# A two-layer decoder trunk on one core: router logits summed by quarter, with edits at the late units, the gated unit and the end

## What is computed

```python
h = rms_norm(x, norm_mix[l]);  parts = split_columns(h @ w_in[l])       # 7176 columns
y_a = moba_attention(q, k, v) @ w_up_moba[l]                            # 8 heads of 64, causal
glu_a, glu_b = jnp.split(gelu(s5_ssm(u, ...)) @ ssm_w_glu[l], 2, axis=-1)
y_b = glu_a * sigmoid(glu_b)                                            # the gated unit
y_c = gated_delta_rule(...) @ w_up_gdn[l]
x = x + (sigmoid(gate_a)*y_a + sigmoid(gate_b)*y_b + sigmoid(gate_c)*y_c) @ w_out[l]
x = x + cross_attention(rms_norm(x, norm_xa[l]), rms_norm(mem, norm_mem[l]), ...)
h = rms_norm(x, norm_ffn[l])
# layer 0: x = x + swiglu(h, ...)
# layer 1, over 8 experts, D_FF = 2816:
logits = h @ w_router;  top_val, top_idx = top_k(logits, 2);  top_w = softmax(top_val)
x = x + sum_e comb[:, e] * swiglu(h, w_gate[e], w_up[e], w_down[e])
# behind the last layer: rms_norm(x, norm_final)
```

## Time and profile before

| | |
|---|---|
| Median of 3 runs | 1755.19 us (1753.54 to 1756.68) |
| The profiled execution's own time | 1754.76 us |
| Its span in the trace | 1753.0 us |
| PE busy | 1696.0 us, 97% |
| DVE busy | 1391.7 us, 79% |
| ACT busy | 1061.0 us, 61% |
| Memory traffic | 434.93 MB, mean 248 GB/s |

### The profile page before, as it was taken

How to read it: one execution, slowest core, us unless ns; L and a number is a source line. 1 busy time by engine, 2 the same in 40 slices (tenths; PEclk the granted TensorE clock), 3 DMA queues, 4 the chain that set the end, 5 groups by cost and what they waited for, 6 DMA issues and landing times. The chain is left out here.

```text
span 1753.0 us, 23683 instructions
## 1 busy us (share of the span) xinstructions
PE 1696.0 (97%) x9485; PEld 1376.7 (79%) x9485; DVE 1391.7 (79%) x1769; ACT 1061.0 (61%) x1228; POOL 160.8 (9%) x218
## 2 busy tenths in 40 slices
PE   8999999999999999999999999999999999999996
PEld 5777767788888888776778788888888888888885
DVE  5798678765555599857875799999998989899996
ACT  4235565565434523566556677777777777777865
POOL 7420002000000333000200100000000000000020
PEclk9999999999999999999999999999999999999998
DMA  8444433355651644453224699999999999999993
GB/s 266 144 145 162 174 119 131 125 192 193 215 173 66 210 145 145 149 187 106 88 101 173 245 395 377 395 372 395 372 396 367 396 387 377 390 374 389 361 395 131
DMA packets 220196, 434.93 MB, mean 248 GB/s; under 512 B 19180, under 2 KB 63864, under 8 KB 220088
## 3 DMA queue, kind: packets, MB, share of 16 engines
q1 hardware_dynamic: 213704, 419.45, 66.4%
q0 software_dynamic: 3520, 11.76, 1.7%
q10 hardware_dynamic: 2864, 2.23, 0.4%
HBM read 422.93 MB, written 10.49 MB: 247 GB/s over the span
## 5 line engine op out<-in xcount | busy, mean ns | idle before, releaser
L1666 DVE TENSOR_TENSOR split_e<-ring,split_e 128x2048 fp32r<-128x2048 f32 x264 | 598.5, 2289 | 40.2 <-ACT split_e L1078 39.9
L1078 ACT ACTIVATE split_e<-ring 128x2048 fp32r<-128x2048 f32 x264 | 503.8, 1921 | 148.7 <-PE bank L3197 127.7
L3195 PE MATMUL bank<-split_e,fx_e 128*128 128x512 f32 x704 | 278.6, 396 | 0.5 <-DVE fx_e L2470 0.5
L3197 PE MATMUL bank<-split_e,fx_e 128*128 128x512 f32 x704 | 274.7, 390 | 0.0
L3196 PE MATMUL bank<-split_e,fx_e 128*128 128x512 f32 x704 | 274.2, 390 | 0.0
L3197 PEld LDWEIGHTS bank<-split_e,fx_e 128*128 128x128 f32 x704 | 132.1, 188 | 28.1
L3195 PEld LDWEIGHTS bank<-split_e,fx_e 128*128 128x128 f32 x704 | 132.2, 188 | 26.7 <-DVE fx_e L2470 0.7
L3196 PEld LDWEIGHTS bank<-split_e,fx_e 128*128 128x128 f32 x704 | 132.4, 188 | 26.2
L3195 PE MATMUL bank<-split_e,f_actT_e 128*128 128x512 f32 x352 | 137.7, 391 | 1.2 <-DVE f_actT_e L2478 1.2
L3197 PE MATMUL bank<-split_e,f_actT_e 128*128 128x512 f32 x352 | 137.0, 389 | 0.0
L3196 PE MATMUL bank<-split_e,f_actT_e 128*128 128x512 f32 x352 | 137.0, 389 | 0.0
(11 more groups left out here) (645 smaller groups left out, 3299.4 us busy)
## 6 DMA issues: line engine op xcount, KB each, us to landing
ring<-in_moe_w_gate SPq DMA_DIRECT2D x40, 2048.0 KB, 13.1
ring<-in_moe_w_up SPq DMA_DIRECT2D x40, 2048.0 KB, 13.1
ring<-in_moe_w_down SPq DMA_DIRECT2D x40, 2048.0 KB, 13.4
ring<-in_w_in SPq DMA_DIRECT2D x27, 2048.0 KB, 8.0
ring<-in_ffn_w_gate SPq DMA_DIRECT2D x11, 1024.0 KB, 5.4
ring<-in_ffn_w_up SPq DMA_DIRECT2D x11, 1024.0 KB, 7.9
ring<-in_ffn_w_down SPq DMA_DIRECT2D x11, 1024.0 KB, 8.8
ring<-in_ssm_w_glu SPq DMA_DIRECT2D x8, 1024.0 KB, 6.2
```

The costliest lines, as they stand in the source:

```text
L1078: nc.scalar.activation(split_e[j % NBUF][:, HI, :], ring[:, s * PIECE + i * HGRP:s * PIECE + (i + 1) * HGRP], ACT.Copy).then_inc(split_hi, 1)
L1666: V.tensor_tensor(split_e[j % NBUF][:, LO, :], ring[:, s * PIECE + i * HGRP:s * PIECE + (i + 1) * HGRP], split_e[j % NBUF][:, HI, :].bitca ...
L3195: mm(bank, a[HI], w[HI], start=first, stop=False)
L3197: return mm(bank, a[LO], w[HI], start=False, stop=last_one)
```

## The change

It has five parts.

1. **Late units.** ACT splits three groups of the next unit, evacuates tile 0, splits the fourth group, evacuates tile 1. A one-element tanh (`warm`) is put behind the second unit. PE's transposes of queries and keys go ahead of the last late unit, ACT's copies of them to behind `late_out` of the unit before last; `mqT` and `mkT` take another place in memory.
2. **Gated unit.** ACT copies `B[0]` as soon as half 0 is summed (step s odd) and takes the tanh of `B[1]` a step later; `glu_th` and `glu_ps` are posted for each half.
3. **Router.** In layer 1 every quarter of the transposes has banks of its own, ACT evacuates it by 128 columns, and PE sums the logits of a quarter right behind the next quarter's transposes, all in `B[2]`. DVE does fewer and wider steps on them. `rstd` is a square root on ACT and a reciprocal on DVE. The two matrices of counts (L3290, L3291) go behind the gathering, and on DVE the split of the gathered tokens goes ahead of the next weight group, the token weights and the row indices.
4. **Last expert.** `flip` goes into the middle of the product before it; the last product sums bank 4 first and posts `y_half`, so that ACT copies bank 4 while PE sums bank 5; its operand lies in `fx_e`. One of two row additions (L2463) moves from chunk 5 to chunk 4.
5. **End.** The sum of squares and the square root are made tile by tile, DVE multiplies `x` by the scale and by the gain in one instruction per tile.

```diff
 for n_ in range(NLATE):
-    unit_split_hi(l, U_LATE + n_ + 1, range(4))
+    unit_split_hi(l, U_LATE + n_ + 1, range(3))
     if n_ == NLATE - 1:
+        unit_split_hi(l, U_LATE + n_ + 1, [3])
         unit_split_hi(l, U_GLU + 1, range(2))
-    late_out(n_)
+    late_out(n_, [0])
+    if n_ < NLATE - 1:
+        unit_split_hi(l, U_LATE + n_ + 1, [3])
+    late_out(n_, [1])
     if n_ == 1:
         table(l, NQ - 1)
+        nc.scalar.activation(warm[:, :], eps_col[:, 2:3], ACT.Tanh)
...
-def glu_tanh(i):
-    act.wait_ge(glu_ps, 4 * l + i + 1)
-    nc.scalar.activation(glu_t[i % 2], B[1][:, :], ACT.Tanh)
+def glu_copy(i):
+    act.wait_ge(glu_ps, 8 * l + 2 * i + 1)
     nc.scalar.activation(glu_y[i % 2], B[0][:, :], ACT.Copy).then_inc(glu_th, 1)
+def glu_tanh(i):
+    act.wait_ge(glu_ps, 8 * l + 2 * i + 2)
+    nc.scalar.activation(glu_t[i % 2], B[1][:, :], ACT.Tanh).then_inc(glu_th, 1)
...
+def router_logits(i):
+    n_, t = i // 2, i % 2
+    for b in range(2):
+        pe.wait_ge(hT_ready, 4 * (3 + 3 * l) + 2 * i + b + 1)
+        for k in (4 * n_ + 2 * b, 4 * n_ + 2 * b + 1):
+            last = mm(B[2][:, t * NE:(t + 1) * NE], hT[:, k, t * P:(t + 1) * P], router_w[:, k, :],
+                      start=k == 0 and t == 0, stop=k == KD - 1 and t == 1)
...
+evac_quarter(0)
+evac_quarter(1)
 act.wait_ge(xo_used, 4 * l + 3)
 squares(x[:, :, :], 0, h_tok, ss)
+nc.scalar.activation(sq_rstd, eps_col[:, 2:3].to_broadcast([P, 2]), ACT.Sqrt)
+evac_quarter(2)
+evac_quarter(3)
...
 gather_matrix(n0)
+gathered_lo(n0)
 if p == 0:
     piece_lo("u", 0, 0, 0)
     token_weights()
-gathered_lo(n0)
-if p == 0:
     row_indices()
...
 def final(p):
     for t in range(NT):
         act.wait_ge(sc_used, 4 * scatters_of_passes(p) - 2 * (NT - 1 - t))
         squares(x[:, :, :], t, h_tok, ss)
-    act.wait_ge(norm_sq, NT * (NNORM + 1))
-    link(nc.scalar.activation(ss, ss, ACT.Ln, scale=1.0 / D, bias=eps_col[:, 0:1]))
-    nc.scalar.activation(rstd, ss, ACT.Exp, scale=-0.5).then_inc(norm_ss, 1)
+        act.wait_ge(norm_sq, NT * NNORM + t + 1)
+        nc.scalar.activation(rstd[:, t:t + 1], ss[:, t:t + 1], ACT.Sqrt, scale=1.0 / D,
+                             bias=eps_col[:, 0:1]).then_inc(norm_ss, 1)
```

More of the change, by code:

```diff
@@ L250, in hybrid_trunk @@
         rm = Region(phase, PH)
-        mqT, mkT = rm.take(KW, SEQ), rm.take(KW, SEQ)
-        m_oT = rm.take(KW, SEQ)
         mp_ = [rm.take(3 * P) for _ in range(2)]
         mpT = [rm.take(3 * P) for _ in range(2)]
-        glu_t = [rm.take(512) for _ in range(2)]
+        glu_t = [rm.take(512)]
+        rm.take(KW, SEQ)
+        glu_t.append(rm.take(512))
         glu_y = [rm.take(512) for _ in range(2)]
+        mqT, mkT = rm.take(KW, SEQ), rm.take(KW, SEQ)
         assert rm.at == 6656
@@ L818, in final @@
                 def final(p):
-                    for t, ready in enumerate((fin_ready, fin_one)):
-                        sp.wait_ge(ready, 1)
+                    for t in range(NT):
+                        sp.wait_ge(fin_ready, t + 1)
                         sp.dma_start(out_d[0, t * P:(t + 1) * P, :], xg[:, t, :]).then_inc(out_done, 16)
@@ L1189, in _, with late_out @@
                         unit_split_hi(l, U_LATE, range(4))
-                def late_out(n_):
-                    for t in range(NT):
+                def late_out(n_, tiles):
+                    for t in tiles:
                         f = F_LATE + 2 * n_ + t
@@ L1219, in _ @@
                             gelu_tanh(q)
[L1220 to L1224, removed]
+                    if n_ == NLATE - 2:
+                        for i in range(4):
+                            act.wait_ge(mtr_ps, 4 * l + i + 1)
+                            dst = (mqT, mkT)[i // 2][:, :, (i % 2) * P:(i % 2 + 1) * P]
+                            nc.scalar.activation(dst, B[4 + i][:, :].rearrange("p (k n) -> p k n", n=P),
+                                                 ACT.Copy).then_inc(mtr_ready, 1)
                 def moba_exp(h):
@@ L2543, in one_pass @@
                                         piece_lo("d", *prev, 1)
-                                if n == NE - 1 and c == NFULL:
-                                    add_rows(range(2, 4))
+                                if n == NE - 1 and c >= 4:
+                                    add_rows([c - 2])
                                 if full:
@@ L2578, in _, with transpose_quarter @@
             tr = nc.tensor.transpose
-            def transpose_quarter(i):
+            def transpose_quarter(i, each=False):
                 n_, t = i // 2, i % 2
+                if each and i >= 2:
+                    pe.wait_ge(hT_ready, 4 * (3 * DEPTH) + 2 * (i - 1))
                 for b in (2 * n_, 2 * n_ + 1):
@@ L2834, in _ @@
                 s5_out(3)
-                for n_ in range(4, NLATE):
+                for n_ in range(4, NLATE - 1):
                     late_unit(n_)
@@ L3226, in down_group @@
                     last.then_inc(split_used, 1)
-                if l % 2 == 1:
-                    pe.wait_ge(tables_in, TABLES)
-                    for k in range(KD):
-                        if k % 2 == 0:
-                            pe.wait_ge(hT_ready, 4 * (3 + 3 * l) + k // 2 + 1)
-                        for t in range(NT):
-                            last = mm(B[t][:, 0:NE], hT[:, k, t * P:(t + 1) * P], router_w[:, k, :],
-                                      start=k == 0, stop=k == KD - 1)
-                    last.then_inc(rl_ps, 1)
                 base = acts_before(l)
@@ L3387, in one_pass @@
                         gather(n0)
+                        if p == 0:
+                            mm(B[3][:, 0:NE], ones[:, :], chosen[:, 0, cols], start=True, stop=False)
+                            mm(B[3][:, 0:NE], ones[:, :], chosen[:, 1, cols], start=False, stop=True).then_inc(rl_ps, 1)
                         for e in range(NE):
@@ L3410, in one_pass @@
                                     gather(n + 1) if by_matrix(n + 1) else turn_rows(n + 1)
-                                if prev is not None:
+                                if closes(n, c):
+                                    output_groups(*prev, between=lambda: flip(n, NFULL))
+                                elif prev is not None:
                                     output_groups(*prev)
```

144 lines of the change are left out of this document (92 added, 52 removed).

## The result

The changed kernel takes 1739.22 us (median of four: 1736.54, 1739.2, 1739.24, 1739.6), beside 1754.37 us of the kernel before in the same session: ratio 0.9907, 95% interval 0.9895 to 0.992. The forecast was 1738.4, between 1734 and 1743.

The account below looks back on a forecast made before the run. PE bounds the experts (93.32 us each), so gains lie outside them: late units -8.2, gated unit -6.0, router +0.5, last expert and end -3.1, sum -16.8; from 1754.76 to 1738.0, median 0.4 higher: 1738.4 us, range 1734 to 1743.

Parts of the forecast that it names:

- rival 3: Late units: the wait was for the fourth split, order gives nothing; 8.2 becomes 4.8, total 1741.8 us; chance 0.09.
- the small waits: Late units: PE's smaller evacuation waits at three following units go, 0.4 us each, 1.2 us per layer.
- the scores: Late units: the first scores no longer wait for ACT's copies of the transposes, 1.1 us gained per layer.
- logits and DVE's steps: Router: idle time ahead of the last transposes goes (-0.4), DVE's dependent steps shrink (-0.6); gathering starts 1.0 us earlier.
- counts in the gap: Router to experts: count records behind the gathering fill PE's 0.53 us wait there, -0.1 us.
- DVE's queue: Expert 0: work moved behind the gathered tokens' split makes PE wait 2.0 us, then another 0.2 at most.
- clock -0.4: Router to gathering: less sparse work makes PE's half-clock drop shorter or absent, 0 to -2.3 us, taken as -0.4.
- The +2.0: Expert 0: price of DVE's late fourth weight group, for which PE waits; between +1.0 and +2.6 us.
- -0.2 for the low part: Last expert: little gained on PE's 1.17 us idle time for the low part, between +0.3 and -1.2 us.
- `flip` earlier doesn't end this alone: Last expert: the low part still stands on DVE behind a weight group, so earlier transposes alone don't end PE's wait.
- the overlap of the transfers: End: first output transfer starts 1.6 us ahead, so the second no longer shares with it; -0.25 us (0 to -0.9).
- rival 4: Memory: DMA can't catch up after DVE's late fourth group, slowing experts; at 358 GB/s 1762 us; chance 0.02.

Follow-up runs that it names:

- e7: Changed kernel with the transposes of queries and keys, and ACT's copies of them, behind the last late unit again: 1740.2 us.
- e5: Changed kernel with the old late-unit order, ACT splitting all four groups ahead of both evacuations; early table load and moved transposes kept: 1741.55 us.
- e6: Changed kernel without the one-element tanh, so the table load stands ahead of the third unit's first evacuation again; new order kept: 1738.01 us.
- e8: Changed kernel with the gated unit as before: ACT does the tanh of bank 1, then the copy of bank 0, behind the second half: 1743.88 us.
- e9: Changed kernel with `flip` behind the product before the last again; row additions stay as changed: 1738.24 us.
- e3: Changed kernel with DVE's scaled tokens and fourth weight group moved ahead of the other token weights and row indices: 1737.9 us.
- e2: Changed kernel with DVE's third weight group and token weights ahead of the split of the gathered tokens again, using the gathering's time: 1735.44 us.
- e10: Changed kernel with both last row additions in the half chunk again; transposes stay in the middle: 1737.91 us.
- e12: Changed kernel with DVE working during the gathering and eight idle PE products, four ahead of the places' sums, four ahead of the gathering: 1732.14 us, ratio 0.9868.
- e4: Changed kernel with eleven idle PE products between logits and gathering, seven ahead of the places' sums, four ahead of the gathering: 1737.07 us.

## Why the prediction was right

**Late units (-8.2, came -8.5): the mechanism right, one split of it wrong.** The evacuation behind the fourth split was what PE waited for, and rival 3 fell. I had given 1.8 us per layer to order and load together, 1.2 to the small waits, 1.1 to the scores. e7 confirms the 1.1 (1.2 and 1.1), e5 the size of the 1.2 (1.33 and 1.43), though at partly other units. e6 shows what I left open: under the new order the load may stay where it was. Of the 4.24 us per layer, 1.4 come back with the old order and 1.15 with the old transposes; the 1.7 that are left are had twice over. 1.4 of them lie at the third unit, where the new order (e6) or the early load (e5) ends the long wait alone. The other 0.3 fit the gap at the last unit, which stays closed in e5 with the old order, most likely by the moved transposes; no run undoes both there. The edit `warm` gives nothing beside the new order.

**Gated unit (-6.0, came -6.6).** e8 gives 3.3 per layer with waits of 5.0 for the copy: 5.7 by rows. The other 0.9, where I had taken 0.3, I put to the heads that start earlier; no run separates it.

**Router to experts (+0.5, came +1.6).** The forecast's own terms, against the traces: logits and DVE's steps -1.0, came -1.73 (start of the gathering, beside that of the output product); counts in the gap -0.1, came -0.32; DVE's queue +2.2, came +2.33, of it 2.04 in the wait; clock -0.4, came **+1.32**. This last one had the wrong sign: I took it that less sparse work ahead of the gathering brings less half clock. The stretch at half clock is as long as before (6.83 us) and starts 0.9 us ahead of the gathering instead of 3.6 ahead, so all of the gathering but its last 0.7 us lies in it. But these are single traces. In e7, e8 and e9, whose code here is that of the changed kernel, the gathering took 5.78, 5.28 and 5.22 us, less than the 5.34 of before in two of them, and expert 0 then 1.5 us more, behind a second stretch at half clock. What the change itself does to the clock stays open; the -0.4 is borne out by none of these traces. The +2.0 was argued as a late fourth group; e3 showed that it is more general, e2 that it was avoidable at no cost.

**Last expert (-1.7, came -2.26).** The scatter as predicted (4.29 to 2.87 us, -1.42). In -0.2 for the low part the step "`flip` earlier doesn't end this alone" was right and went too far: what stands on DVE was moved as well, and both together gave 0.86, of which either one alone gives 0.1 to 0.2 (e9, e10).

**End (-1.4, came -2.45).** The steps ahead of the second transfer were right: 3.0 us instead of 4.2. Mis-sized was the overlap of the transfers, 0.25 taken and 1.3 in the trace (second tile written to the end: 6.2 before, 4.9 after, 4.4 to 5.5 in the twelve traces with this end); my bound of 0.9 did not hold it.

The sum is 1.4 us short of the profiled execution, whose -18.2 holds +1.1 at the router against -0.3, -0.6, -0.5 and -1.1 elsewhere. Against the medians (-15.2 in the first session, -16.1 in the second) the -16.8 is somewhat too much, and that it lies so near is in part luck: the router's loss was too small in the forecast and every gain was too small too, so the errors offset each other; I had put the median 0.4 us above a profiled execution, and for the changed kernel it lay 2.7 and 0.3 above.

One sum of rival 4 was wrong: with 34.6 MB per expert, 358 GB/s mean 96.7 us for each, 27 us more over eight, so 1765 us and not 1762. Nothing hangs on it, since the experts keep their 93.32 us in every trace.

The rule of the Trainium skill that I had weighed ("ScalarE: Activation LUTs", section "What ACT_TABLE_LOAD costs": a drain of 1.38 us beside the load) isn't seen here either. In e6 the load begins at 144.55 and the evacuation at 145.84, 1.29 us behind it; over all table loads of the fourteen traces the median from the load's start to the next instruction's is 1.29 us too. And the logits, ahead of which the change puts a load, came earlier than forecast, not later.

## What to carry to other kernels

Before instructions on a queue are put in another order, write down what the engine did in the idle time that the new order makes: here 5.35 us of DVE's work left the cover of the gathering and came back as a wait of 2 us, at whichever of two groups it was put (e3), while the order that used the cover gained 2.6 us. Two fixes for one stall often replace each other instead of adding up (early load and new order) or need each other (transposes and row addition); undoing each alone tells which. Where an engine waits between dense stretches, look at the granted clock of the stretch behind the wait and not only at the wait. And before a difference of some tenths between two traces is put down to an edit, look at the same stretch in the traces whose edit lies elsewhere: the last expert and the transfers differ by up to 1 us between them.

## What the runs showed of the hardware

The 32 records of one gathering took 3.84 us at full clock (granted 1.00, 2.4 GHz) and 6.66 where all but the last 0.7 us lay at half (0.50, 1.2 GHz). Of the thirteen traces behind the change, twelve have a stretch at half clock, 3.4 to 10.2 us long, that begins 4.8 to 0.3 us ahead of the gathering; only e12, where PE stands idle for 0.7 us at most between the logits and the gathering, has none (e4 had that time filled too, but its fall came ahead of the products). The same kernel had 6.8 us of it in one trace and 10.2 in another, which by itself moves the time by 0.6 us.

In four traces (e4, e7, e8 and e9) a second stretch of 3.4 us begins in expert 0, 0.7 to 1.3 us behind the end of PE's wait of 2 us for DVE, and expert 0 takes 97.3 us instead of 95.75. In the two kernels without that wait none does, nor in the other seven traces with it. So it may be that such a wait costs more than itself, but it isn't shown as the cause: in three of the four (e4, e8, e9) the first stretch was 3.4 us instead of 6.8 or more, so that the two together are no longer than the one of the changed kernel.

A table load on ACT took 1.28 us, and where it stood ahead of an evacuation with room, as in e6, it cost PE 0.1 us or less. Two transfers of the output that were issued together ended the span 9.9 us behind the last addition (10.4 before); with the first issued 1.4 us ahead of the second it was 7.4 to 8.5.
